# Opening by channel halves: the first adaLN modulation in two halves, and half of the SSM tiles' products ahead of the second half

## The chip, the core and the metric

One core of one Trainium2 chip runs the whole layer. The metric is the device time of one execution in microseconds (us), the median of the runs. Engines: TensorE (PE) multiplies and transposes, VectorE (DVE) and ScalarE (ACT) work element by element, GpSimd (POOL) splits weights, SyncE (SP) issues most DMAs; ACT issues DMAs too, in the order of its own instructions.

## What is computed

One decoder block on x (2048 rows of 1024 channels, float32), cut to what matters here:

```
c_act = silu(c)
sh1, sc1, g1, sh2, sc2, g2 = split(c_act @ w_ada + b_ada, 6)
h = rmsnorm(x, norm1_g) * (1.0 + sc1) + sh1
u_conv, u_ssm, gl_conv, gl_ssm = split(h @ w_in, ...)
y_conv = conformer_conv(u_conv, ...)
y_ssm = s5_mixer(u_ssm, a, b, c, d, log_dt, w_glu)
merged = sigmoid(gl_conv) * y_conv + sigmoid(gl_ssm) * y_ssm
x = x + g1 * (merged @ w_out)
h = rmsnorm(x, norm2_g) * (1.0 + sc2) + sh2
x = x + g2 * (swiglu(h @ w_ffn_in) @ w_ffn_out)
out = rmsnorm(x, final_g)
```

Nothing can be multiplied by `w_in` before `sh1` and `sc1` are known, and those need 8 MB of `w_ada`. This wait at the very beginning is the opening.

## The kernel before

The sequence is worked through in four blocks of 512 rows (mixers), then the feed-forward network in a second part that the change doesn't touch. Every float32 product is made of three: operand and weight are each split into a high part (fp32r) and the rest, and `three` (L1925) issues high x high, high x low, low x high. POOL makes the two parts of each 512 KB weight chunk (`w_hi`, L2255; `w_lo`, L2259) out of three raw buffers into two split slots. Each engine's order is written out by hand, and named steps on semaphores (`pe_pro`, L365; `act_pro`, L385) tie them.

The opening before, in the program's names:

- SP (L2313) issues eight 1 MB slabs of `w_ada` (`ada`, L2317), each one of two kinds (shift or scale), a half of the 1024 channels, and a half of the 1024 rows of the product. Then come three weight chunks (`raw`, L2367), small parameters (`load_small`), then further chunks.
- ACT issues the vectors (c, biases, gains; `nat_v`, L1263), x (`xs`, L1257), the SSM poles, `log_dt` and the B parameters (L1298 to L1302).
- `c` is turned by PE, copied to `vt` by DVE, and put through Silu by ACT (step `cs`). DVE puts it into `zc` (L658).
- Slabs 0, 2 and 4 are weighted and summed by DVE (`slab_sum`, L667 and L669); slabs 1, 3, 5, 6 and 7 go through PE (`modulation_rows`, L1852: four matmuls a slab, each recorded as two passes). PE adds DVE's sums (L1864), DVE copies the four rows of the result (`modrow`, L690), PE turns them (step `mt`, L1869), and DVE adds the bias and makes `scale0` (L693, L650, L652).
- PE turns x into eight channel tiles (`transposes`, L1882), with 32 small transposes of the B parameters between tile 3 and tile 4 (step `bx`, L1892). For each tile ACT makes the modulated high part and the full value (`h_tile`, L1292), and DVE the rest (`h_split`, L620).
- Then PE makes the four SSM input tiles `us0` to `us3`, each over all eight channel tiles (24 products), in order. ACT copies each one out (`uz`, L1391), stores it (L1395) and issues the loads that bring it back turned (`ssm_turn`: eight DMA issues a tile, L1400). In its program these stand as us0, us1, turn 0, us2, turn 1, us3, turn 2, turn 3. Behind them stand the sigmoid of the first convolution gate (L1406) and eight copies of the state matrices (L1324).
- PE goes on with two convolution input tiles (`ua0`, `ug0`) and the state matrices (`state_matrix`: L1906, L1911). Their transposes go through three banks, so PE waits there for ACT's copies. They read `wm`, which DVE builds after its last `h_split`, up to the copy of `cwt` (L752).

Of the kernel before, what the change touches and what calls it, by code (L numbers as in the profile page):

```python
# [45 lines left out]
def build(nc, x, c, w_ada, b_ada, norm1_g, w_in, conv_w, conv_b, conv_ln_g, conv_ln_b, conv_proj,  # L46
# [38 lines left out]
    FIRST_CHUNKS = [ssm_chunks + sum(conv_chunks, [])]  # L85
# [76 lines left out]
    with ExitStack() as ctx:  # L162
# [125 lines left out]
        def early(at, end, *buffers):  # L288
# [6 lines left out]
        jarg, jtmp, nat_v, nat_a, nat_w, iota_i, iota_f, cx = early(  # L295
            ssm_at, yn_at, ("jarg", [P, 2, T + 1, G]), ("jtmp", [P, T + 1, G]), ("nat_v", [nv_rows, P]),
            ("nat_a", [2 * G, P]), ("nat_w", [KC * TAPS, P]), ("iota_i", [P, NC + 1], I32),
            ("iota_f", [P, NC + 1]), ("cx", [P, 2, 4, P]))
# [5 lines left out]
        sv, jexp, jer, jei, b1, ptmp, modrow, zc, dvec, ddiag, zt, one_row, turns = early(  # L304
            mc_at, ms_at, ("sv", [P, 12, G]), ("jexp", [P, T + 1, G]), ("jer", [P, T + 1, G]),
            ("jei", [P, T + 1, G]), ("b1", [P, G, HG]), ("ptmp", [P, G, HG]), ("modrow", [4, HALF]),
# [4 lines left out]
            (ync_at, ync_at + 8192, ync_at + 16384, ms_at, ms_at + 8192, turn_at, turn_at + 8192, h_at))]  # L311
# [53 lines left out]
        pe_pro = ["v1", "ada1", "v0", "ada3", "ada5", "ada6", "ada7", "sums", "mt"] + h_steps[0:4] + ["bx"] + h_steps[4:] + ["v2"]  # L365
# [19 lines left out]
        act_pro = ["cs", "dt"] + norm_act + [f"nx{i}" for i in R(TT)] + ["ej", "m8", "sj", "cj"] + h_act  # L385
# [49 lines left out]
        for st, names in [("pro", pe_pro)] + list(enumerate(pe_mix)):  # L435
            z = 0
            for n in names:
                if n[:2] == "oc" or n[0] == "v" or n in ("bx", "sums"):
                    continue
                if st != "pro" and n[0] == "h":  # L440
                    plan[st, n] = 4 + int(n[1]) % 4
                elif is_z(n) or n[:2] == "o0":
                    plan[st, n] = z % 4
                    z += 1
# [105 lines left out]
        vectors_in = sem("vectors_in")  # L550
# [18 lines left out]
        for b, names in enumerate(pe_mix):  # L569
            chunk_used.append([tensor.after(b, n) for n in names if n[:2] in ("us", "gl", "ua", "ug", "oc")  # L570
# [8 lines left out]
        def _(dve):  # L579
# [34 lines left out]

            def wait_self(stage, name):
                dve.wait_ge(*vec.after(stage, name))
# [38 lines left out]
            dve.wait_ge(*tensor.after("pro", "v1"))  # L655
            link(v.tensor_copy(vt[:], bank[1][:, 0:nv_rows]), "vt")
            dve.wait_ge(*scal.after("pro", "cs"))
            link(v.tensor_copy(zc[:, :, 3], cact), "zc")  # L658

            def slab_sum(n):  # L660
                _, half, rows = SLABS[n]
                sums = acc[:, half * HALF:(half + 1) * HALF]
                dve.wait_ge(ada_in[n % ADA], 16 * (n // ADA + 1))
                for j in R(KD // 2):
                    k = rows * KD // 2 + j
                    if k == 0:
                        link(v.tensor_scalar(sums, ada[n % ADA][:, j, :], cact[:, k:k + 1], None, ALU.mult))  # L667
                    else:
                        link(v.scalar_tensor_tensor(out=sums, in0=ada[n % ADA][:, j, :], scalar=cact[:, k:k + 1],  # L669
                                                    in1=sums, op0=ALU.mult, op1=ALU.add),  # L670
                             f"slab{n}" if j == 3 else None)

            slab_sum(0)
            slab_sum(2)
            norm_mean("pro")
            slab_sum(4)
            norm_root("pro")
            dve.wait_ge(*tensor.after("pro", "v0"))
            link(v.tensor_copy(sv[:, 0:2, :].rearrange("p a g -> p (a g)"), bank[0][:, 0:2 * G]))
# [3 lines left out]
            link(v.tensor_tensor(lg, dt, ar, ALU.mult))  # L683
            link(v.tensor_tensor(jexp[:], iota_f[:, 0:T + 1].unsqueeze(2).broadcast_to([P, T + 1, G]),
                                 lg.unsqueeze(1).broadcast_to([P, T + 1, G]), ALU.mult))
            link(v.tensor_tensor(th, dt, ai, ALU.mult))
            reduce_angle(th, th, t0)
            angles(jarg[:, 0, :, :], jarg[:, 1, :, :], jtmp[:], th, T + 1, "jargs")
            dve.wait_ge(*tensor.after("pro", "sums"))
            link(v.tensor_copy(modrow[:], bank[7][0:4, :]), "modrow")  # L690
            dve.wait_ge(*tensor.after("pro", "mt"))
# [560 lines left out]
        def _(act):  # L1252
# [65 lines left out]
            for k in R(KD):  # L1318
                h_tile("pro", k, 0)
# [1243 lines left out]
```

## Time and profile before

| | |
|---|---|
| median of 3 runs | 2531.41 us (2530.98 to 2531.72) |
| profiled execution | 2529.16 us |
| span of its trace | 2527.4 us |
| PE busy | 2485.8 us, 98% |
| POOL busy | 1722.3 us, 68% |
| DVE busy | 1649.6 us, 65% |
| ACT busy | 876.1 us, 35% |

The busy share is an average over the span; the opening is its first 90 us. The chain of waits follows the work that ended last back from the end: each piece released the next, or stood before it on its engine. The timeline lists instructions by start. In both, a row begins with the start in us and the length in us; ACTq and SPq are queues that issue DMAs.

### The profile page before, as it was taken

How to read it: one execution, taken by the hardware profiler on the slowest of the kernel's cores; microseconds unless marked ns; L12 is line 12 of the kernel's file. 1: busy time of each engine (PE TensorE's matmuls, PEld its weight loads, DVE VectorE, ACT ScalarE, POOL GpSimd, SP SyncE). 2: the span in 40 equal slices, each digit the busy share in tenths (PEclk: the TensorE clock that was granted, in tenths of full speed). 3: DMA queues.
4: the chain of work that ended last, by engine and by line, in shares of the span. 5: the costliest groups of instructions: out<-in, count | busy, mean ns of one | idle time of the engine just before them, and what ended most of it. 6: DMA issues, size and time to landing. Idle time of an engine off the chain costs nothing.

```text
span 2527.4 us, 31370 instructions
## 1 busy us (share of the span) xinstructions
PE 2485.8 (98%) x11419; PEld 2047.8 (81%) x11419; DVE 1649.6 (65%) x2038; ACT 876.1 (35%) x1379; POOL 1722.3 (68%) x1182
## 2 busy tenths in 40 slices
PE   7999999999999999999999999999999999999998
PEld 3888788888888888888788888878888888888886
DVE  5899639946596648946833334385554326799798
ACT  4322421153012421146533345443323334445444
POOL 2777777677866777675787767788778764445545
PEclk9999999999999999999999999999999999999999
DMA  8676357553666347462332232325566327465533
GB/s 281 203 196 217 117 166 219 153 168 120 214 170 192 126 158 225 137 223 92 122 96 76 79 115 90 109 76 158 175 188 196 100 83 253 148 221 189 198 96 121
DMA packets 426161, 395.66 MB, mean 157 GB/s; under 512 B 92232, under 2 KB 330520, under 8 KB 424472
## 3 DMA queue, kind: packets, MB, share of 16 engines
q1 hardware_dynamic: 324688, 319.93, 40.5%
q10 hardware_dynamic: 101320, 73.72, 9.5%
q8 instruction: 92, 1.51, 0.2%
q14 instruction: 61, 0.50, 0.1%
HBM read 317.88 MB, written 67.24 MB: 152 GB/s over the span
## 4 chain that ended last, share of the span: by engine, by line
PE 84%; DVE 7%; DMA 3%; issue 2%; ACT 2%; POOL 1%; ACTq 1%; SPq 1%; POOLq 0%; DVEq 0%
PE bank L1927 19%; PE bank L1929 19%; PE bank L1928 19%; PE bank L2172 5%; PE bank L2173 5%; PE bank L2174 5%; DMA row_pair<-in_w_ffn_out 2%; PE bank L2086 2%; PE bank L2088 2%; PE bank L2087 2%; DVE bank L1027 1%; PE bank L2007 1%; PE bank L2006 1%; PE bank L1992 1%; DMA ada<-in_w_ada 1%
## 5 line engine op out<-in xcount | busy, mean ns | idle before, releaser
L2259 POOL TENSOR_TENSOR w_lo<-raw,w_hi 128x1024 fp32r<-128x1024 f32 x192 | 479.8, 2499 | 36.6 <-ACT w_hi L1385 12.5
L2255 POOL CAST w_hi<-raw 128x1024 fp32r<-128x1024 f32 x186 | 199.6, 1073 | 345.0 <-PE bank L1929 271.3
L1927 PE MATMUL bank<-h_hi,w_hi 128*128 128x512 f32 x896 | 351.8, 393 | 0.9 <-ACT wm L1324 0.9
L1929 PE MATMUL bank<-h_hi,w_lo 128*128 128x512 f32 x896 | 349.4, 390 | 0.0
L1928 PE MATMUL bank<-h_lo,w_hi 128*128 128x512 f32 x896 | 349.1, 390 | 0.0
L839 DVE SCALAR_TENSOR_TENSOR bank<-uc,cwt,bank 128x512 f32<-128x512 f32 x464 | 323.1, 746 | 6.2
L2282 POOL TENSOR_TENSOR fw_lo<-fsum,fw_hi 128x512 fp32r<-128x512 f32 x176 | 237.8, 1354 | 75.8 <-ACT fw_hi L1617 75.8
L1927 PE MATMUL bank<-xc_hi_T,fw_hi 128*128 128x512 f32 x704 | 276.4, 393 | 8.0 <-DVE tr L1032 6.5
L1929 PE MATMUL bank<-xc_hi_T,fw_lo 128*128 128x512 f32 x704 | 274.8, 390 | 0.0
L1928 PE MATMUL bank<-xc_lo_T,fw_hi 128*128 128x512 f32 x704 | 274.7, 390 | 0.0
L2309 POOL TENSOR_TENSOR ow_lo<-raw,ow_hi 128x512 fp32r<-128x512 f32 x116 | 161.8, 1395 | 163.1 <-ACT ow_hi L1664 163.1
L2172 PE MATMUL bank<-ow_hi,hid_hi 128*128 128x512 f32 x616 | 240.1, 390 | 3.2 <-POOL ow_lo L2309 3.1
L2174 PE MATMUL bank<-ow_lo,hid_hi 128*128 128x512 f32 x616 | 239.7, 389 | 0.0
L2173 PE MATMUL bank<-ow_hi,hid_lo 128*128 128x512 f32 x616 | 239.6, 389 | 0.0
L2282 POOL TENSOR_TENSOR fw_lo<-raw,fw_hi 128x512 fp32r<-128x512 f32 x110 | 156.0, 1419 | 80.7 <-ACT fw_hi L1617 80.6
L1927 PE MATMUL bank<-xc_hi_B,fw_hi 128*128 128x512 f32 x528 | 206.3, 391 | 2.4 <-DVE xc_lo_B L823 2.4
L1929 PE MATMUL bank<-xc_hi_B,fw_lo 128*128 128x512 f32 x528 | 205.5, 389 | 0.0
L1928 PE MATMUL bank<-xc_lo_B,fw_hi 128*128 128x512 f32 x528 | 205.4, 389 | 0.0
L1927 PEld LDWEIGHTS bank<-h_hi,w_hi 128*128 128x128 f32 x896 | 168.7, 188 | 35.6 <-issue 1.3
L1929 PEld LDWEIGHTS bank<-h_hi,w_lo 128*128 128x128 f32 x896 | 168.6, 188 | 35.7
L1928 PEld LDWEIGHTS bank<-h_lo,w_hi 128*128 128x128 f32 x896 | 168.7, 188 | 34.4
L1617 ACT ACTIVATE fw_hi<-fsum 128x512 fp32r<-128x512 f32 x176 | 110.8, 629 | 222.7 <-PE bank L1929 121.0
(341 smaller groups left out, 5242.8 us busy)
## 6 DMA issues: line engine op xcount, KB each, us to landing
raw<-in_w_in SPq DMA_DIRECT2D x112, 512.0 KB, 3.9
raw<-in_w_ffn_in SPq DMA_DIRECT2D x66, 512.0 KB, 5.7
hid_scratch<-tr SPq DMA_DIRECT2D x88, 256.0 KB, 3.2
raw<-tsum_scratch SPq DMA_DIRECT2D x66, 256.0 KB, 3.2
g2b<-in_w_ada SPq DMA_DIRECT2D x64, 256.0 KB, 3.7
ssm_m<-vk_scratch SPq DMA_DIRECT2D x32, 512.0 KB, 5.1
raw<-in_ssm_glu SPq DMA_DIRECT2D x32, 512.0 KB, 3.9
raw<-in_w_out SPq DMA_DIRECT2D x32, 512.0 KB, 3.6
```

What stands on the lines that cost most here:

```text
L839: ins = v.scalar_tensor_tensor(out=dst, in0=src, scalar=w, in1=conv_bank(m)[:], op0=ALU.mult, op1=ALU.add)
L1617: s.activation(fw_hi[i][:], src, ACT.Copy).then_inc(whi_done, 1)
L1927: t.matmul(dst, wh, xh, start=first, stop=False)
L1928: t.matmul(dst, wh, xl, start=False, stop=False)
L1929: return t.matmul(dst, wl, xh, start=False, stop=last)
L2172: t.matmul(dst, hid_hi[h][:, cols], ow_hi[w][:], start=(k == 0), stop=False)
L2173: t.matmul(dst, hid_lo[h][:, cols], ow_hi[w][:], start=False, stop=False)
L2174: return t.matmul(dst, hid_hi[h][:, cols], ow_lo[w][:], start=False, stop=(k == KH2 - 1))
L2255: g.tensor_copy(hi[:], src[:]).then_inc(hi_done, 1)
L2259: g.tensor_tensor(lo[:], src[:], hi[:].bitcast(F32), ALU.subtract).then_inc(split_done, 1)
L2282: g.tensor_tensor(fw_lo[i][:], part[WEIGHTS[i]], fw_hi[i][:].bitcast(F32), ALU.subtract)\
L2309: g.tensor_tensor(ow_lo[n % OW][:], fraw[n % 4][:, 0:HALF], ow_hi[n % OW][:].bitcast(F32), ALU.subtract)\
```

## The change

The slabs of the first channel half (0 to 3) are loaded and reduced first, giving shift and scale of channel tiles 0 to 3 (`scale00`); the second half (slabs 4 to 7, `scale01`) follows. The weights of the SSM tiles are cut anew: a chunk holds two SSM tiles (256 columns) over one half of the channel tiles. PE makes the products of us0 and us1 over channel tiles 0 to 3 (step `A0`), then slab 5 and the B transposes, then us2 and us3 over tiles 0 to 3 (`A1`), with the sums of the second half inside. After the second half's modulation `ssm_rest` makes us0 and us1 over tiles 4 to 7, then us2 and us3. Slabs 6 and 7 go from PE to DVE. ACT loads c alone and `log_dt` first, then x, then the vectors. A Silu on a constant stands ahead of the one on c.

```
-    FIRST_CHUNKS = [ssm_chunks + sum(conv_chunks, [])]
+    FIRST_CHUNKS = [[("us", pair_, half) for half in range(2) for pair_ in range(KS // 2)] + sum(conv_chunks, [])]
...
-        pe_pro = ["v1", "ada1", "v0", "ada3", "ada5", "ada6", "ada7", "sums", "mt"] + h_steps[0:4] + ["bx"] + h_steps[4:] + ["v2"]
+        pe_pro = ["vc", "ada1", "v1", "v0", "ada3", "sums0", "h0", "h1", "mt0", "h2", "h3", "A0", "ada5", "bx", "sums1", "A1",
+                  "mt1", "h4", "h5", "h6", "h7", "v2"]
...
-        act_pro = ["cs", "dt"] + norm_act + [f"nx{i}" for i in R(TT)] + ["ej", "m8", "sj", "cj"] + h_act
+        act_pro = ["pre", "cs", "dt"] + norm_act + [f"nx{i}" for i in R(TT)] + h_act[:2 * KH] + ["ej", "m8", "sj", "cj"]
+        act_pro += h_act[2 * KH:]
...
             slab_sum(0)
...
+            dve.wait_ge(*tensor.after("pro", "v1"))
+            for cols in (slice(0, 6 * KD), slice(7 * KD, nv_rows)):
+                link(v.tensor_copy(vt[:, cols], bank[7][:, cols]), "vt")
             dve.wait_ge(*tensor.after("pro", "v0"))
...
+            slab_sum(2)
+            norm_mean("pro")
...
+            modulation_half(0)
+            for k in R(KH):
+                h_split("pro", k)
+                slab_step(4, k)
+            slab_sum(6)
+            slab_sum(7)
...
+            modulation_half(1)
...
+            def ssm_products(pair_, k):
+                pe.wait_ge(*vec.after("pro", f"hl{k}"))
+                hi, lo = (w[pair_][:].rearrange("p (k n) -> p k n", n=2 * P) for w in (w_hi, w_lo))
+                for j in R(2):
+                    m, cols = 2 * pair_ + j, slice(j * P, (j + 1) * P)
+                    ins = three(bank[plan[0, f"us{m}"]][:], hi[:, k % KH, cols], lo[:, k % KH, cols],
+                                h_hi[:, k, :], h_lo[:, k, :], k == 0, k == KD - 1)
+                    if k == KD - 1:
+                        ins.then_inc(*tensor.step(0, f"us{m}"))
+                return ins
...
+            ssm_products(1, 0)
+            ssm_products(1, 1)
+            modulation_sums(1, [(0, "slab6", 1), (1, "slab7", 0)])
+            ssm_products(1, 2)
+            ssm_products(1, 3).then_inc(*tensor.step("pro", "A1"))
+            modulation_turn(1)
+            transposes("pro", 4)
+            pe.wait_ge(pro_v, mark["scale01"])
+            transposes("pro", 5)
+
+            def ssm_rest():
+                pe.wait_ge(split_done, RAW + 3)
+                for k in R(KH, KD):
+                    if k == KD - 1:
+                        pe.wait_ge(taps_in, 16 * KC)
+                        pe.wait_ge(*vec.after("pro", "hl7"))
+                        turn_rows_in(2, nat_w, bank[7])
+                    ssm_products(0, k)
+                    if k < KH + 2:
+                        transposes("pro", k + 2)
+                pe.wait_ge(split_done, RAW + 4)
+                for k in R(KH, KD):
+                    ssm_products(1, k)
...
-                    ssm_input(*R(KS))
+                    ssm_rest()
                     conv_input(0)
```

**PE, from the start to the first SSM product, before** (`nat_v` vectors, `ada` slabs, `nat_a` poles, `one_row` DVE's sums, `modrow` the modulation's rows, `xs` the transposes of x, `nat_b` the B parameters):

```order
L1841 MATMUL bank<-ident,nat_v 128x84
L1852 MATMUL bank<-ada_225,zc 4x512 x4
L1841 MATMUL bank<-ident,nat_a 128x64
L1852 MATMUL bank<-ada_227,zc 4x512 x4
L1852 MATMUL bank<-ada_229,zc 4x512 x4
L1852 MATMUL bank<-ada_230,zc 4x512 x4
L1852 MATMUL bank<-ada_231,zc 4x512 x4
L1864 MATMUL bank<-acc,one_row 4x512 x2
L1869 MATMUL bank<-ident,modrow 128x4 x4
L1882 MATMUL bank<-ident,xs 128x128 x16
L1892 MATMUL bank<-ident,nat_b_205 128x32 x16
...
L1927 MATMUL bank<-h_hi,w_hi_52 128x512
```

and in the change (a buffer's number may differ by one between the two; `ada_226` is slab 1):

```order
L1898 MATMUL bank<-ident,nat_c 128x8
L1879 MATMUL bank<-ada_226,zc 2x512 x4
L1870 MATMUL bank<-ident,nat_v 128x84
L1870 MATMUL bank<-ident,nat_a 128x64
L1879 MATMUL bank<-ada_228,zc 2x512 x4
L1886 MATMUL bank<-acc,one_row 2x512
L1918 MATMUL bank<-ident,xs 128x128 x8
L1893 MATMUL bank<-ident,modrow_217 128x2 x4
L1918 MATMUL bank<-ident,xs 128x128 x4
L1924 MATMUL bank<-h_hi,w_hi_52 128x512
```

Two slabs and one sum stand ahead of the first modulation in place of five and two, and products stand right behind three tiles' transposes.

**PE, between `A0` and the second half, in the change** (`w_hi_53` is the second split slot, with us2 and us3; the runs of 12 products each are shown by their first rows):

```order
L1879 MATMUL bank<-ada_230,zc 2x512 x4
L1945 MATMUL bank<-ident,nat_b_206 128x32 x16
L1945 MATMUL bank<-ident,nat_b_207 128x32 x16
L1924 MATMUL bank<-h_hi,w_hi_53 128x512
...
L1886 MATMUL bank<-acc,one_row 2x512 x2
...
L1893 MATMUL bank<-ident,modrow_233 128x2 x4
L1918 MATMUL bank<-ident,xs 128x128 x8
```

All of it now stands ahead of the transposes of channel tiles 4 to 7, which before followed the B transposes directly.

**SP, from the start, in the change** (before, the eight slabs stood ahead of `raw_49`, `raw_50` and `raw_51`):

```order
L2399 DMA ada_225<-in_w_ada 128x4x512
L2399 DMA ada_226<-in_w_ada 128x4x512
L2399 DMA ada_227<-in_w_ada 128x4x512
L2399 DMA ada_228<-in_w_ada 128x4x512
L2456 DMA raw_49<-in_w_in 128x4x256
L2456 DMA raw_50<-in_w_in 128x4x256
L2399 DMA ada_229<-in_w_ada 128x4x512
```

Two weight chunks moved ahead of four slabs.

## Rows read from the trace of the kernel before

**Rows 1.** The page, busy time of TensorE: busy us, share of the span, instructions.
```profile
PE 2485.8 (98%) x11419; PEld 2047.8 (81%) x11419; DVE 1649.6 (65%) x2038; ACT 876.1 (35%) x1379; POOL 1722.3 (68%) x1182
```
**Rows 2.** Chain of waits, 0 to 150 us: start us, us, what.
```profile
6.32 21.90 DMA ada<-in_w_ada
28.26 10.46 PE bank L1852 x24
...
43.58 3.64 PE bank L1892 x32
...
67.31 1.14 ACT uz L1391
...
72.28 1.67 ACTq L1400
...
83.26 1.28 ACT L1406
...
85.15 3.93 ACT wm L1324 x8
89.21 0.47 PE bank L1927
...
140.23 0.43 PE bank L1928
```
**Rows 3.** Timeline of ACT and its queue in the opening.
```profile
28.63 4.27 ACT L1311 ACTIVATE xs<-xs,rs 128x1024 f32<-128x1024 f32 x4 [2.55 <-DVE rs L630]
...
42.41 0.78 ACT L1292 ACTIVATE h_hi<-bank,mod,scale 128x512 fp32r<-128x512 f32 x1 [5.46 <-DVE scale L652]
...
56.42 1.14 ACT L1391 ACTIVATE uz<-bank 128x512 f32<-128x512 f32 x1 [2.70 <-PE bank L1929]
...
63.41 3.85 ACTq L1400 DMA_DIRECT2D u<-us_scratch  x8
...
75.53 7.70 ACTq L1400 DMA_DIRECT2D u<-us_scratch  x16
```
**Rows 4.** Timeline of DVE in the opening.
```profile
11.51 0.17 DVE L658 COPY zc<-vt 128x8 f32<-128x8 f32 x1 [2.28 <-ACT vt L1305]
...
16.32 3.11 DVE L669 SCALAR_TENSOR_TENSOR acc<-ada,vt,acc 128x512 f32<-128x512 f32 x4 [1.75 <-DMA ada<-in_w_ada]
...
40.55 0.68 DVE L690 COPY modrow<-bank 4x512 f32<-4x512 f32 x1 [6.79 <-PE bank L1864]
...
43.93 0.69 DVE L620 TENSOR_TENSOR h_lo<-bank,h_hi 128x512 fp32r<-128x512 f32 x1 [0.35 <-ACT bank L1292]
...
53.76 0.69 DVE L620 TENSOR_TENSOR h_lo<-bank,h_hi 128x512 fp32r<-128x512 f32 x1 [0.58 <-ACT bank L1292]
...
75.57 0.29 DVE L752 COPY cwt<-bank 128x124 f32<-128x124 f32 x1
```
**Rows 5.** Timeline of TensorE (PEld: its weight loads) in the opening.
```profile
11.74 5.94 PE L1852 MATMUL bank<-ada,zc 128*4 128x512 f32 x8 [2.87 <-DVE zc L658]
...
22.50 0.09 PEld L1852 LDWEIGHTS bank<-ada,zc 128*4 128x4 f32 x2 [4.74 <-DMA ada<-in_w_ada]
...
41.28 0.41 PE L1869 MATMUL bank<-ident,modrow 4*128 4x4 f32 x4 [0.84 <-DVE modrow L690]
41.62 1.97 PE L1882 MATMUL bank<-ident,xs 128*128 128x128 f32 x16
...
50.65 0.48 PE L1927 MATMUL bank<-h_hi,w_hi 128*128 128x512 f32 x1
...
83.43 1.03 PE L1906 MATMUL bank<-ident,cx 128*128 128x128 f32 x8
```
**Rows 6.** Timeline of POOL: the first weight chunk's cast.
```profile
34.94 1.04 POOL L2255 CAST w_hi<-raw 128x1024 fp32r<-128x1024 f32 x1 [32.09 <-DMA raw<-in_w_in]
```
**Rows 7.** Busy us (x) of PE, PEld, DVE, ACT, POOL; granted clock; DMA share, GB/s.
```profile
48.00:49.00 1.00, 1.00 (x7) 1.00 (x6) 0.93 (x3) 0.71 (x2) 0.00 (x0) 0.50 1.06 309
...
140.00:141.00 1.00, 1.00 (x4) 0.77 (x3) 0.97 (x2) 0.33 (x1) 1.00 (x2) 0.50 1.28 287
```

More of the change, by code:

```diff
@@ L653, in scale_of, with slab_step @@
                                      ALU.mult), f"scale{which}")
-            dve.wait_ge(*tensor.after("pro", "v1"))
-            link(v.tensor_copy(vt[:], bank[1][:, 0:nv_rows]), "vt")
             dve.wait_ge(*scal.after("pro", "cs"))
             link(v.tensor_copy(zc[:, :, 3], cact), "zc")
+            def slab_step(n, j):
+                kind, half, rows = SLABS[n]
+                part = (half + kind) % 2
+                sums = acc[:, part * HALF:(part + 1) * HALF]
+                k = rows * KD // 2 + j
+                if j == 0:
+                    dve.wait_ge(ada_in[n % ADA], 16 * (n // ADA + 1))
+                if k == 0 or n == 7 and j == 0:
+                    link(v.tensor_scalar(sums, ada[n % ADA][:, j, :], cact[:, k:k + 1], None, ALU.mult))
+                else:
+                    link(v.scalar_tensor_tensor(out=sums, in0=ada[n % ADA][:, j, :], scalar=cact[:, k:k + 1],
+                                                in1=sums, op0=ALU.mult, op1=ALU.add),
+                         f"slab{n}" if j == KD // 2 - 1 else None)
@@ L660, in slab_sum @@
             def slab_sum(n):
-                _, half, rows = SLABS[n]
-                sums = acc[:, half * HALF:(half + 1) * HALF]
-                dve.wait_ge(ada_in[n % ADA], 16 * (n // ADA + 1))
                 for j in R(KD // 2):
[L665 to L671, printed above, removed]
+                    slab_step(n, j)
@@ new lines, in _ @@
+            transposes("pro", 0)
+            transposes("pro", 1)
+            modulation_turn(0)
+            pe.wait_ge(*scal.after("pro", "cs"))
+            transposes("pro", 2)
+            pe.wait_ge(split_done, RAW + 1)
+            for k in R(KH):
+                if k == 1:
+                    transposes("pro", 3)
+                ins = ssm_products(0, k)
+            ins.then_inc(*tensor.step("pro", "A0"))
+            pe.wait_ge(pro_v, mark["vt"])
+            modulation_rows(5)
+            parameter_rows()
@@ L1923, in kernel_tiles @@
                     ins.then_inc(*tensor.step(0, f"kk{n}"))
-            def three(dst, wh, wl, xh, xl, first, last):
-                t.matmul(dst, wh, xh, start=first, stop=False)
-                t.matmul(dst, wh, xl, start=False, stop=False)
-                return t.matmul(dst, wl, xh, start=False, stop=last)
             def mixers(b, last=False):
-                chunk = [0]
+                chunk = [0 if b else KS]
                 def next_chunk():
@@ L2314, in _, with load_slab @@
         def _(sp):
-            for n, (kind, half, rows) in enumerate(SLABS):
+            def load_slab(n):
+                kind, half, rows = SLABS[n]
                 col = kind * D + half * HALF
@@ L2318, in _ @@
                     .then_inc(ada_in[n % ADA], 16)
+            for n in R(4):
+                load_slab(n)
             def load_small():
```

176 lines of the change are left out of this document (99 added, 77 removed).

## The prediction

> **What bounds the kernel now.** The page's busy shares come first: TensorE is busy 98% of the span [rows 1], so the change can only move idle or slow time of TensorE, and it touches nothing but the opening. The second view is the chain of waits over the first 150 us [rows 2]; the reader should watch who holds it. Up to 28.3 us it is the landing of the adaLN slabs, then 24 passes of slabs on PE (10.46 us, 0.436 each), then transposes, among them the 32 small ones of the B parameters (3.64 us). PE multiplies without a gap from 50.65 to 83.43 us [rows 5], but the chain leaves it at 67.31 for ACT: the copy of us2, its turning loads, us3, 16 more load issues up to 83.26, a sigmoid, eight state-matrix copies [rows 2, 3]. Only at 89.21 does PE go on. So two runners arrive at the state matrices almost together: PE at 83.43, ACT at 83.26 and with 6 us of work to do there. The prediction is about which of them the change helps.
>
> An opening that is x us shorter or longer shifts all that follows by x, since from 89.21 the chain is PE again and every later load, copy and split is timed by PE's steps.
>
> **The front: modulation of half the channels.** ACT issues one more DMA ahead (0.48, an eighth of a turn's 3.85) and a second Silu; c no longer waits for the other vectors. DVE's `zc`, 11.51 before, comes at about 12.4 [rows 3, 4]. x now comes in beside slabs 0 and 1, so I take 12.7 for slab 1 on PE (between 12.4, nothing lost, and 13.4). Slab 1 takes 5.94 [rows 5], to 18.6; the vectors and the poles are turned and copied behind it, 1.3, to 19.9. Seven small DVE operations at about 0.22 (a copy of 8 columns is 0.17 [rows 4], the rest handover), which stood later before, end at 21.4. Slab 2 on DVE is 3.11 [rows 4], to 24.5; mean, root, four small operations and the reciprocal take 1.4 at the same price, to 25.9. The scaling of x, 4.27 [rows 3], ends at 30.2; it began at 28.63 before, so this part gains 2.7. Slab 3 lands as before (22.5; the same bytes stand ahead of it [rows 5]) and was through at the latest when slab 5 began at 28.26 [rows 2]; with the sum that is 29.1, so x decides. Eight transposes are 1.0 (16 in 1.97), the turn 0.41 [rows 5], the copy of the rows lies beside the scaling (0.68 [rows 4]), bias and scale 0.6: ACT's first modulated tile starts at 32.4 against 42.41 [rows 3]. **Ten microseconds are won here**, and it is the last place where something is won. Slabs 4 to 7 are hidden now, and so are slabs 6 and 7, which leave PE (16 passes, 7.0 us) for DVE: eight operations at 0.78 behind the fourth rest end near 47, when PE is not yet at the sum.
>
> **First products (A0).** From ACT's first instruction on a tile to the end of DVE's rest is 2.2 us (42.41 to 43.93 + 0.69 [rows 3, 4]): 34.6. A product takes 0.228 on average (144 between 50.65 and 83.43 [rows 5]), six a channel tile 1.37. The transposes of tile 3 stand behind the first six, end at 36.5, and its rest is ready at 38.8; A0 would end at 40.2. But TensorE has stood nearly idle from 29 to 34.6, and the rows show what that does: behind the small transposes the granted clock is 0.50 [rows 7], 1.2 in place of 2.4 GHz, and there a product takes 0.43 [rows 2, 7]. I count one such spell, about nine products at 0.2 more: +1.8, A0 ends at 42.0. Bounds: none, 0; all 24 products, +4.9. The chunk for A0 is no wait: before it landed behind eight slabs at 34.94 [rows 6]; with half of the 8 MB behind it, it is some 10 us earlier, and POOL has nothing else to do.
>
> **What now stands between the two halves.** PE's order is fixed: slab 5, 8 x 0.436 = 3.5, to 45.5; B transposes 3.64, to 49.1 [rows 2]; 12 products 2.7, to 51.9; the sums, four passes, 1.7, to 53.6; 12 products 2.7, which cover the copy of the rows, to 56.3; turn 0.41, bias and scale 0.7, to 57.4. Then 2.2 for tile 4: 59.6. Before, the last tile, tile 7, was ready at 54.45 [rows 4].
>
> **The end of the SSM tiles.** Six products of tile 4 (1.37) and four transposes (0.5) stand ahead of ACT's tile 6, and the same again ahead of tile 7: 59.6 + 3.7 = 63.4, + 2.2 = 65.6 for the last rest. With the taps' transpose (0.3) and three products us0 is complete at **66.4; before, ACT took it at 56.42** [rows 3]. PE has 27 products left, 6.2, to 72.6, and 48 of the convolution tiles, 10.9: 83.5, what it was (83.43). PE neither gains nor loses.
>
> **ACT's queue decides.** Before, us0, us1, us2 and us3 came 5.5 us apart and ACT worked in between. Now us0 and us1 come together at 66.4 to 67.1 and all of its work stands behind: four copies and stores at 1.55 (1.14 for the copy [rows 3], and one issue, somewhat under a turn's 0.48), 6.2, and 32 issues, 3.85 + 3.85 + 7.70 = 15.4 [rows 3]: 66.5 + 21.6 = 88.1. Once in four turns one issue stood 1.67 in place of 0.45 [rows 2]; with that, 89.3. Before it was 83.26: **+4.8 or +6.1**. I take the latter, as the issues now stand closer together. The 6 us of sigmoid and state-matrix copies follow unchanged, so PE goes on at 95.3 in place of 89.21. DVE is late too, but less: from the last rest to `cwt` 21.4 (54.45 to 75.86 [rows 4]), so 87.0.
>
> The Trainium skill has a rule against such an order: "TensorE: Matmul & The Clock Gate", section "HAM oscillation — how this bites in real kernels", says that matmuls in short bursts between waits run at the low clock burst after burst. The trace agrees for one spell [rows 7]; that it recurs in every burst no row shows.
>
> **Sum.** The profiled execution took 2529.16, 2.3 below the median of 2531.41; +6.1 gives 2535.3 for such an execution and **2537.5** for the median. Changes below 0.2% (5.1 us) can't be told from none here.
>
> **The rivals.**
> - The same mechanism, but PE stays at the high clock or ACT's loads are issued without a stall: +3.1 to +4.9, about 2535.5. For it: the level stays up through shorter idle stretches. Against: 6 us with hardly a matmul. Chance 0.26.
> - **Not slower: a quick front.** If slab 1 runs at the high clock (3.5 in place of 5.94), all that hangs on the scaling of x comes 2.4 earlier; with no low spell (1.8) and no stall (1.2) us0 is complete at 62.2 and ACT free at 83.9: +0.7, 2532.1. It decides where us0 comes before 61.7; beyond that the gain is real. For it: slab 1's eight passes took 0.74 each, slab 5's 0.436 [rows 5, 2], so there is that much to win. Against: all three must hold. Chance 0.12, and 0.04 for more than 5 us faster, for which us0 would have to stand at 56.
> - Two low spells (A0 and behind the B transposes, where the trace has one [rows 7]), or the chunk for A0 late by 4, as if it didn't get ahead of the slabs: +8.5 to +10.5, about 2541. Chance 0.07.
> - Low clock in every burst: all 48 early products at 0.43 cost 9.7, 1.8 of them counted: +14, 2545.5. It is what the page's rule would make of it. Chance 0.03.
>
> The forecast itself, +5.1 to +8.5, has 0.48. Slower by over 0.2%: 0.48 + 0.07 + 0.03 = 0.58. Within: 0.26 + 0.12 = 0.38. Faster: 0.04. The range, 2531 to 2542, holds the first three cases and nearly all of the fourth; what it leaves out is about 0.12.
>
> **What would show it.** Right: first modulated tile near 32.4, A0 ending at 40 to 42, last rest at 64 to 67, us0's copy near 66.5, the turn issues without a wait between them up to 88 or 89, PE waiting some 5 to 6 us for ACT's state-matrix copies, and the trace from there the old one, shifted. Wrong: us0's copy before 62, PE at the state matrices later than ACT, or a chain of waits that doesn't pass through the turn issues. If the shift at the state matrices isn't the shift at the end, something later has slack that I didn't see.

## The result, and the profile after

The changed kernel takes **2552.88 us** (2550.18 to 2553.61) against 2531.29 (2530.98 to 2531.72) before: 1.0083 times, interval 1.0071 to 1.0096, 21.6 us slower. Slower was forecast, but by 6.1, and the time lies beyond the range. The profiled execution, the fastest of the four, has a span of 2548.3 us, 20.9 more than before. The page still has TensorE busy nearly all the time; the place to look is the opening.

The page's first row of the changed kernel:

```profile
PE 2489.6 (98%) x11410; PEld 2053.2 (81%) x11410; DVE 1674.1 (66%) x2051; ACT 876.7 (34%) x1380; POOL 1720.0 (67%) x1182
```

PE's timeline shows where the shift arises (start, duration, work, and in brackets the idle time before it and what ended it; L1918 transposes x, L1879 multiplies slabs, L1945 turns the B parameters, L1886 sums, L1924 multiplies):

```profile
35.08 1.97 PE L1918 MATMUL bank<-ident,xs 128*128 128x128 f32 x8 [4.98 <-ACT xs L1337]
...
40.63 0.77 PE L1924 MATMUL bank<-h_hi,w_hi 128*128 128x512 f32 x1 [2.02 <-DVE h_lo L629]
...
48.46 3.60 PE L1879 MATMUL bank<-ada,zc 128*2 128x512 f32 x8
51.99 3.73 PE L1945 MATMUL bank<-ident,nat_b 32*128 32x32 f32 x32
55.65 0.80 PE L1924 MATMUL bank<-h_hi,w_hi 128*128 128x512 f32 x1
...
61.07 2.06 PE L1886 MATMUL bank<-acc,one_row 128*2 128x512 f32 x4
...
72.02 0.77 PE L1924 MATMUL bank<-h_hi,w_hi 128*128 128x512 f32 x1 [3.87 <-DVE h_lo L629]
...
108.71 0.47 PE L1924 MATMUL bank<-h_hi,w_hi 128*128 128x512 f32 x1 [0.91 <-ACT wm L1353]
```

The first product stands at 40.63 where 50.65 was before [rows 5]: ten microseconds earlier, but six later than forecast. From there the lead is lost piece by piece, and PE's first product behind the state matrices comes at 108.71 in place of 89.21 [rows 2], **+19.5**. Another 1.5 is added where the state matrices are first used, around 153 to 163; from 298.88 (before 277.86) to the end the shift stays at 21. So 19.5 of the 21 are lost in the first 108 us.

What stands between the last rest and PE's next product is short to read. From DVE's timeline:

```profile
78.90 0.69 DVE L629 TENSOR_TENSOR h_lo<-bank,h_hi 128x512 fp32r<-128x512 f32 x1 [1.03 <-ACT bank L1316]
79.63 0.69 DVE L755 TENSOR_TENSOR b<-bank,sv 128x512 f32<-128x512 f32 x1
...
100.84 0.29 DVE L774 COPY cwt<-bank 128x124 f32<-128x124 f32 x1
```

and from ACT's:

```profile
94.68 7.72 ACTq L1429 DMA_DIRECT2D u<-us_scratch  x16
102.43 1.28 ACT L1435 ACT_TABLE_LOAD   x1 [8.17 <-issue]
```

The last rest ends at 79.59, 14.0 later than forecast. DVE needs 21.9 from its start to `cwt`, ACT has its four turns until 102.4; they end 1.3 apart, ACT last, and ACT's sigmoid and state-matrix copies follow. PE waits 3.42 for `cwt` up to 101.18, and then only 0.29 and 0.91 for ACT's copies. The tail behind the last rest was predicted: from its end to PE's next product 95.3 - 65.6 = 29.7 forecast, 108.71 - 79.59 = 29.1 measured. What stands ahead of it was not.

### What holds DVE

DVE's timeline of the changed kernel, where the first modulation is prepared:

```profile
25.81 0.88 DVE L634 TENSOR_SCALAR ss<-ss 128x4 f32<-128x4 f32 x1
26.61 0.18 DVE L710 TENSOR_TENSOR sv<-sv 128x32 f32<-128x32 f32 x1
26.82 2.32 DVE L711 TENSOR_TENSOR sv<-sv 128x32 f32<-128x32 f32 x1
29.18 0.94 DVE L712 TENSOR_TENSOR sv<-sv 128x32 f32<-128x32 f32 x1
30.16 0.35 DVE L713 RECIPROCAL sv<-sv 128x32 f32<-128x32 f32 x1
30.55 0.18 DVE L639 RECIPROCAL rs<-sd 128x4 f32<-128x4 f32 x1
30.64 2.18 DVE L715 TENSOR_TENSOR jexp<-iota_f,sv 128x288 f32<-128x288 f32 x1
```

and POOL's at the same time, casting and subtracting the first weight chunks:

```profile
25.41 1.26 POOL L2336 CAST w_hi<-raw 128x1024 fp32r<-128x1024 f32 x1 [22.56 <-DMA raw<-in_w_in]
26.76 2.34 POOL L2340 TENSOR_TENSOR w_lo<-raw,w_hi 128x1024 fp32r<-128x1024 f32 x1
29.04 1.04 POOL L2336 CAST w_hi<-raw 128x1024 fp32r<-128x1024 f32 x1
30.16 2.34 POOL L2340 TENSOR_TENSOR w_lo<-raw,w_hi 128x1024 fp32r<-128x1024 f32 x1
```

Three operations of equal size, L710 to L712, take 0.18, 2.32 and 0.94. The long ones end with POOL's operation: 26.82 + 2.32 = 29.14 against 26.76 + 2.34 = 29.10, and 29.18 + 0.94 = 30.12 against 30.08. They don't run slowly beside POOL; they wait for it. The two reciprocals, with one tensor to read, run beside POOL's second subtraction at the length that they have alone (0.35 and 0.18; in the run with the splits held, 0.35 and 0.18). Before, POOL's first cast came at 34.94 [rows 6], when DVE stood idle up to 40.55 [rows 4], so none of the rows read from before shows the clash. The change brings the chunk ten microseconds forward, into DVE's busiest stretch.

The Trainium skill, "SBUF — State Buffer", section "Who interferes with whom", states this as an exclusive lock on ports that the two engines share: a DVE instruction with two SBUF inputs contends with a GpSimd instruction that reads SBUF, and a DVE instruction with at most one SBUF input does not, unless it runs in a mode that uses both ports; of such a mode it says that the one that issues first keeps the ports for its whole instruction while the other is blocked. The rows above agree: the two ends above lie within 0.05 us, the reciprocals are free, and the one-input TENSOR_SCALAR L634, a form that by the section can run in such a mode, waits for the cast (25.81 + 0.88 against 25.41 + 1.26). The prediction did not weigh this section.

The second clash stands at tile 4's rest:

```profile
67.48 2.22 DVE L732 TENSOR_SCALAR sv<-jer 128x32 f32<-128x32 f32 x1
69.73 0.97 DVE L733 TENSOR_TENSOR sv<-sv 128x32 f32<-128x32 f32 x1
...
71.19 0.69 DVE L629 TENSOR_TENSOR h_lo<-bank,h_hi 128x512 fp32r<-128x512 f32 x1
```

```profile
67.30 2.35 POOL L2340 TENSOR_TENSOR w_lo<-raw,w_hi 128x1024 fp32r<-128x1024 f32 x1
69.62 1.03 POOL L2317 TENSOR_TENSOR acc<-g2b,vt 128x512 f32<-128x512 f32 x1
```

Four small operations, 0.2 each elsewhere, stand ahead of the rest on DVE. Two of them take 3.2, one up to the end of the subtraction of POOL's fourth split (69.65), the other up to the end of POOL's next operation (70.65); PE waits 3.87 for the rest.

### What the clock does

Windows of the changed kernel (busy us and counts of PE, PEld, DVE, ACT, POOL; granted clock; DMA share; GB/s):

```profile
34.00:44.00 10.00, 6.90 (x26) 5.50 (x27) 6.65 (x14) 5.12 (x7) 0.00 (x0) 0.51 0.84 262
44.00:54.00 10.00, 10.00 (x47) 6.10 (x45) 7.84 (x8) 5.42 (x8) 3.77 (x2) 0.98 1.00 309
54.00:62.00 8.00, 8.00 (x30) 5.56 (x30) 2.80 (x5) 0.00 (x0) 0.00 (x0) 0.57 0.20 59
...
71.00:76.00 5.00, 3.98 (x13) 3.24 (x14) 2.12 (x7) 0.44 (x1) 0.00 (x0) 0.66 0.49 154
...
100.00:106.00 6.00, 4.52 (x26) 4.12 (x27) 5.69 (x10) 3.35 (x5) 4.80 (x4) 0.72 0.64 175
...
153.00:163.00 10.00, 9.42 (x38) 8.94 (x39) 9.90 (x13) 2.23 (x4) 8.40 (x6) 0.53 0.90 238
```

The prediction counted one spell at 1.2 GHz, at the first products. There are three in the products (34 to 44, 55 to 61, 72 to 75) and one more at the state matrices' transposes (100 to 106). The price of the three by rows: transposes 1.97 in place of 1.0 and about seven products at 0.43 (the rest of A0 at 0.228); the first twelve products of A1 5.42 in place of 2.7; some six of tile 4.

### The profile page after: what moved, and what is told of

It reads as the page before. It is cut to its first block, busy times and chain, and to the rows that moved or that the text cites. A ratio compares the mean times of both kernels' runs of the same rounds, so it can differ in the third digit from the quotient of the medians.

```text
span 2548.3 us, 31381 instructions
## 1 busy us (share of the span) xinstructions
PE 2489.6 (98%) x11410; PEld 2053.2 (81%) x11410; DVE 1674.1 (66%) x2051; ACT 876.7 (34%) x1380; POOL 1720.0 (67%) x1182
## 4 chain that ended last, share of the span: by engine, by line
PE 83%; DVE 9%; DMA 3%; issue 2%; ACT 2%; POOL 0%; ACTq 0%; SPq 0%; POOLq 0%; DVEq 0%
PE bank L1924 19%; PE bank L1926 19%; PE bank L1925 19%; PE bank L2254 5%; PE bank L2253 5%; PE bank L2255 5%; DMA row_pair<-in_w_ffn_out 2%; PE bank L2167 2%; PE bank L2169 2%; PE bank L2168 2%; PE bank L2088 1%; PE bank L2073 1%; PE bank L2087 1%; DVE bank L1049 1%; DVE stage L841 1%
## 5 line engine op out<-in xcount | busy, mean ns | idle before, releaser
L1924 PE MATMUL bank<-h_hi,w_hi 128*128 128x512 f32 x896 | 354.7, 396 | 7.3 <-DVE h_lo L629 6.4
L1924 PE MATMUL bank<-xc_hi_T,fw_hi 128*128 128x512 f32 x704 | 276.1, 392 | 8.5 <-DVE tr L1054 7.1
L1924 PE MATMUL bank<-xc_hi_B,fw_hi 128*128 128x512 f32 x528 | 206.3, 391 | 2.5 <-DVE xc_lo_B L845 2.5
L1924 PEld LDWEIGHTS bank<-h_hi,w_hi 128*128 128x128 f32 x896 | 169.9, 190 | 43.8 <-issue 8.7
```

What stands on the lines that cost most here:

```text
L1924: t.matmul(dst, wh, xh, start=first, stop=False)
```

## The experiments

Each run was timed beside the kernel before on the same chip. The kernel before had a median of 2531.29 beside the change; 2529.42 beside the next four runs of the table; 2531.40 beside "no early products", "splits held, turns late" and the two "slab 6" runs without a held split; and 2530.09 beside the other four. So ratios compare better than times. "Last rest" is the start of tile 7's rest on DVE, "PE goes on" PE's first product behind the state matrices; both from each run's profile, while the time is the median of several executions, so small differences between neighbours mean little; that of "B transposes between products" took 2557.28, 6 above its median.

| kernel | time, us | ratio to before (interval) | last rest | PE goes on |
|---|---|---|---|---|
| before | 2531.29 | | 53.76 | 89.21 |
| changed | 2552.88 | 1.0083 (1.0071 to 1.0096) | 78.90 | 108.71 |
| POOL's splits held back | 2545.77 | 1.0064 (1.0049 to 1.0079) | 71.27 | 103.61 |
| DVE's order | 2549.44 | 1.0079 (1.0064 to 1.0094) | 73.58 | 105.71 |
| B transposes between products | 2551.19 | 1.0082 (1.0066 to 1.0099) | 81.56 | 112.36 |
| filler matmuls | 2551.46 | 1.0087 (1.0072 to 1.0102) | 76.95 | 109.68 |
| no early products | 2547.77 | 1.0064 (1.0050 to 1.0078) | 58.49 | 100.48 |
| splits held, turns late | 2542.10 | 1.0042 (1.0026 to 1.0057) | 71.50 | 101.95 |
| halves only, mended | 2542.70 | 1.0048 (1.0035 to 1.0062) | 61.57 | 98.78 |
| the same, splits held, turns late | 2540.50 | 1.0038 (1.0024 to 1.0052) | 60.24 | 97.77 |
| early products, all aids | 2547.54 | 1.0073 (1.0057 to 1.0088) | 72.15 | 100.17 |
| before, slab 6 on DVE | 2533.13 | 1.0006 (0.9998 to 1.0015) | 54.90 | 90.77 |
| the same, turns late | 2533.91 | 1.0016 (1.0007 to 1.0025) | 53.48 | 89.72 |
| slab 6 on DVE, split held | 2533.56 | 1.0008 (1.0000 to 1.0017) | 51.92 | 90.45 |

**POOL's splits held back.** Of the changed kernel, on POOL:

```diff
                     pool.wait_ge(raw_in[w % RAW], 16 * (b * (NW // RAW) + w // RAW + 1))
+                    if b == 0 and w == 0:
+                        pool.wait_ge(pro_v, mark["jargs"])
+                    if b == 0 and w == 3:
+                        pool.wait_ge(*vec.after("pro", "hl5"))
```

> POOL holds its first split back until DVE has the angles (step jargs), and the fourth until the rest of channel tile 5; nothing else is changed. Theory that DVE's small SBUF operations wait while POOL splits weights: the 2.34, 0.95 and 2.18 us of operations that elsewhere take 0.2 to 0.5 shrink to that, the scaling of x starts about 3.5 earlier (27.2 in place of 30.76), the rest of channel tile 4 follows its ACT output at once instead of 2 us later; together 4.5 to 6 us less than the change (2552.9), about 2547.5. Theory that those operations are long for a reason of their own (a handover, a DMA): no gain, or a loss of up to 3 us, because the weights of the first early products come later.

DVE's and POOL's timelines of this run:

```profile
25.90 0.19 DVE L711 TENSOR_TENSOR sv<-sv 128x32 f32<-128x32 f32 x1
26.13 0.19 DVE L712 TENSOR_TENSOR sv<-sv 128x32 f32<-128x32 f32 x1
...
26.84 0.43 DVE L715 TENSOR_TENSOR jexp<-iota_f,sv 128x288 f32<-128x288 f32 x1
```

```profile
30.43 1.04 POOL L2340 CAST w_hi<-raw 128x1024 fp32r<-128x1024 f32 x1 [27.58 <-DVE jarg L619]
```

The same operations take 0.19, 0.19 and 0.43 in place of 2.32, 0.94 and 2.18, and the last rest comes 7.6 earlier. It is the clash that cost this, and the time, 16.4 over its own runs of before in place of 21.6, fell by the 4.5 to 6 expected. Part of the clash only moved: POOL's splits, now behind the angles, hold the two operations that make the scale, which took 0.17 and 0.16 in the change.

```profile
33.01 0.92 DVE L693 TENSOR_SCALAR scale<-mod 128x4 f32<-128x4 f32 x1
33.96 0.94 DVE L694 TENSOR_TENSOR scale<-scale,vt 128x4 f32<-128x4 f32 x1
```

PE goes on only 5.1 earlier, because here ACT ends last: its turns run to 96.4 with `cwt` ready at 93.49.

**DVE's order.** POOL as in the change; DVE's pole operations go behind slab 7, and tile 4's and 5's rests ahead of the small operations:

```diff
-            link(v.tensor_tensor(den, t0, t1, ALU.add))
-            link(v.reciprocal(den, den))
...
             slab_sum(7)
+            link(v.tensor_tensor(den, t0, t1, ALU.add))
+            link(v.reciprocal(den, den))
...
+            h_split("pro", 4)
+            h_split("pro", 5)
             link(v.tensor_scalar(nr, e_r, -1.0, None, ALU.add))
```

> Only DVE's order: the four operations on the poles go from ahead of the root's reciprocal to behind slab 7, and the rests of channel tiles 4 and 5 go ahead of the six small operations; POOL is as in the change. Theory that operations on DVE are held up while POOL splits: the reciprocal of the root (four columns) comes behind the mean directly, near 27 in place of 30.55, unless it is held up itself, and tile 4's rest ends 2 us sooner: 4 to 6 us less than the change, about 2548. The held-up time then turns up in the next operations, the angles, where it costs nothing up to 35. If only the order counts and not POOL, the gain is the plain length of the moved operations, 1.0 + 0.9 us.

Scaling of x starts at 26.96 in place of 30.76, but the angles are now what waits (jexp, with two SBUF inputs, 2.36; L606, a TENSOR_SCALAR, 2.35), and `modrow` comes at 34.99 (35.86 in the change). PE goes on 3.0 earlier than in the change; the intervals of the two ratios overlap, so the expected 4 to 6 are not shown. A new order among DVE's operations moves the wait to the next one.

**B transposes between products.** They are issued eight at a time, ahead of each of A1's first four triples of products, so that no stretch holds small transposes alone:

```diff
-            parameter_rows()
+            eight = parameter_rows()
...
-            ssm_products(1, 0)
-            ssm_products(1, 1)
+            ssm_products(1, 0, eight)
+            ssm_products(1, 1, eight)
```

> The 32 small B transposes go in groups of eight between the first four groups of three products of us2 and us3, in place of one run of 32 ahead of them. Theory that the run lets the granted clock fall: it stays at 1.00 from 45 on, the twelve products take 0.228 in place of 0.43 and the four passes of the sums 0.436 in place of up to 0.85; PE is at the turn of the second half 3.0 us earlier; 3 to 4 us less than the change, about 2549.5. Theory that the clock falls there for what went before: no gain within 1 us.

Windows of this run:

```profile
45.00:55.00 10.00, 10.00 (x44) 5.64 (x42) 9.68 (x11) 3.55 (x6) 3.73 (x2) 1.00 0.96 295
55.00:65.00 10.00, 10.00 (x30) 4.70 (x29) 1.27 (x3) 0.00 (x0) 0.00 (x0) 0.50 0.01 3
```

The low clock came all the same, at 55, and stayed through the sums. Mixing did not keep it away, and the time stayed that of the change; the idea fell.

**Filler matmuls.** Seven slab matmuls whose result nobody reads, ahead of A0:

```diff
+            filler(5)
             transposes("pro", 0)
...
             transposes("pro", 2)
+            filler(2)
```

> Seven matmuls of 512 columns into a bank that is not yet in use are added: five ahead of the transposes of channel tile 0, two behind those of tile 2, where PE waits for ACT and DVE. Theory that idling lets the clock fall ahead of the early products: granted clock 1.00 up to 52, eight transposes 1.0 in place of 1.97, the first nine products 0.228 in place of 0.43, A0 ends 2.5 to 3.5 us earlier, and the total falls by as much, about 2550. If the first early products are paced by ACT and DVE anyway, A0 ends at most 1 us earlier. If the fillers themselves delay, up to 1 us slower.

The granted clock stays at 1.00 from 27 to 53, A0 ends 2.05 earlier (slab 5 at 46.41 against 48.46), and the last rest 1.95 earlier. So about 2 is what the first spell costs. At the state matrices it is spent again: 0.52 from 98 to 108, where the change had 0.83; PE goes on 1.0 later, and the time did not fall.

**No early products.** The halves stay; the us tiles stand whole behind the second, as before:

```diff
-            pe.wait_ge(split_done, RAW + 1)
-            for k in R(KH):
-                ins = ssm_products(0, k)
...
-            ssm_products(1, 0)
-            ssm_products(1, 1)
...
-                    ssm_rest()
+                    ssm_input(*R(KS))
```

> The modulation stays in two halves, but no product is multiplied ahead of the second half: the us tiles stand whole behind it, in the order of the kernel before. If the early products are what is lost (they run at the low clock in short bursts, and the four us tiles come together, so that DVE and ACT have everything still to do behind the last rest): slab 5 follows the transposes of tile 3 on PE at about 38 to 39, sums near 48, tile 4's rest near 56, the last rest near 61 in place of 78.90, products without a gap from 56 on, first tile past the state matrices near 95 (before 89.21, after 108.71), time 5 to 8 over the kernel before, about 2537. If the split of the modulation itself costs the time (DVE held beside POOL's splits at the front, sums over half the channels twice), the last rest comes no earlier than 70 and the time stays over 2545.

The last rest comes 20 earlier than in the change and PE goes on 8.2 earlier, though this edit had a fault of its own: the taps' transpose waited for the last rest ahead of all products and held them to 59.46. The time, 16.4 over the kernel before, is far from the 5 to 8 expected.

**Splits held, turns late.** The run with POOL's splits held, and on ACT:

```diff
-                    ssm_turn(2)
-                    ssm_turn(3)
                     sigmoid_u(0)
                     state_matrix()
+                    ssm_turn(2)
                     angle_turns()
                     sigmoid_u(1)
+                    ssm_turn(3)
```

> The run with POOL's first splits held back, with one thing more: ACT's third and fourth turn (two copies and 24 load issues) stand behind the state-matrix copies. Queue theory: in the run with the splits held back, cwt was ready at 93.20 but ACT issued turning loads up to 96.42 and copied from 97.7; now ACT is free near 84, the copies start near 95.5 and PE's next products come 2 to 4 earlier than at 103.61: time about 2543. If DVE's state matrices alone decide, or the loads are needed sooner than they now come, no gain: 2545 to 2547, with a new wait for u in the stage at 150 us.

PE goes on 1.7 earlier than with the splits alone, a little under the 2 to 4 expected, and the time, 2542.10, is close to the 2543 of the queue theory: ACT's turns are part of the tail as soon as DVE is early enough. PE now waits for `cwt` again, 3.42 up to 93.78, and the state matrices' transposes behind it take 1.97 and 5.50 where the kernel before had 1.03 and 4.00: the granted clock is 0.50 from 93 to 98. From PE's start on them to its next product it is 8.2 here and was 5.8 before, so 2.4 of the gain went there.

**Halves only, mended.**

```diff
-            turn_rows_in(2, nat_w, bank[7])
...
                             pe.wait_ge(*vec.after("pro", f"hl{k}"))
+                            if k == KD - 1:
+                                turn_rows_in(2, nat_w, bank[7])
```

> The run without early products once more, with one fault of its own mended: there the turning of the taps waited for the last rest ahead of all products, and held the first from about 55 to 59.46; now it stands ahead of the eighth channel tile's products. If that wait was on the path: first product near 56, us0 3 earlier, PE's next products after the state matrices at 97 to 98 in place of 100.48, time about 2544. If DVE's front and the low clock are all that is left of the loss: no change at 2547.

PE's timeline of this run:

```profile
59.66 0.78 PE L1923 MATMUL bank<-h_hi,w_hi 128*128 128x512 f32 x1
...
93.11 1.03 PE L1973 MATMUL bank<-ident,cx 128*128 128x128 f32 x8
93.98 3.90 PE L1978 MATMUL bank<-ident,wm 128*128 128x128 f32 x32
98.78 0.47 PE L1923 MATMUL bank<-h_hi,w_hi 128*128 128x512 f32 x1 [0.91 <-ACT wm L1352]
```

The first product is no earlier than with the fault (expected near 56): in this execution POOL's first split again held the pole operations (2.32 and 0.94), the scaling of x began at 30.83, and the last rest came 3.1 later than in the run before. From 59.66 to 93.11 PE doesn't wait once; `cwt` (83.51) and ACT's turns (to 91.9) are hidden behind it. This is the comparison that decides: **the change without its early products costs 9.6, the early products another 9.9** (98.78 - 89.21, 108.71 - 98.78; by the medians, each against its own runs of before, 12.6 and 9.0). The first part is not the halves alone: the new order of loads and slabs 6 and 7 on DVE belong to it, and the clash at the front. The second holds the weight chunks' new cut as well.

**The same, splits held, turns late.** Both edits from above on this one.

> The run before this one with POOL's first split held until the angles are done and ACT's third and fourth turn behind the state-matrix copies. Port theory: the angles of 288 columns, which took 2.01, 1.17 and 2.35 beside POOL's splits, take 0.46 and 0.31 again, modrow stands 3 earlier than 34.60, the first modulated tile near 33.5, the last rest near 56; with the queue out of the way PE's next products after the state matrices come at 92 to 94, time 2535 to 2537: the split of the modulation alone, at its best, 4 to 6 over the kernel before. If halving the modulation were worth its name, it would come under 2531.

The scaling of x starts 3.9 earlier (26.97 against 30.83), the last rest only 1.3. Windows of this run and, for the same stretch, of the run with halves only:

```profile
46.00:60.00 14.00, 11.42 (x45) 6.94 (x45) 7.50 (x21) 5.38 (x8) 0.00 (x0) 0.52 0.53 166
```

```profile
46.00:60.00 14.00, 11.19 (x58) 7.53 (x58) 9.40 (x23) 5.31 (x9) 0.00 (x0) 0.67 0.62 190
```

Most of the gain at the front was given back, in two parts. The splits, now behind the angles, hold DVE's two scale operations here too (0.93 and 0.94 in place of 0.17 and 0.16), 1.5. And PE's slab 5 (5.95 in place of 4.92) and sums (3.57 in place of 2.9) run at the low clock for longer, about 1.5 as well. The expected 2535 to 2537 was missed by 3.5.

**Early products, all aids.** Held splits, DVE's order, fillers and late turns in the changed kernel.

> The changed kernel, early products and all, with every aid that gained in its opening: POOL's splits 0 and 3 held back, DVE's pole operations behind slab 7 and tile 4's and 5's rests ahead of the small operations, seven filler matmuls ahead of the first products, ACT's third and fourth turn behind the state-matrix copies. If the losses add up as named (port 5, clock at the first products 2, queue 2 to 3): last rest near 68 in place of 78.90, PE's next products at 98 to 100 in place of 108.71, time 2539 to 2541, so still over the run without early products. If the low clock only moves to another place when it is driven out of one: no better than 2542.1, the run with splits and turns alone.

PE goes on at 100.17, close to the 98 to 100 expected, but the last rest, 72.15, missed the 68, because the aids get in each other's way. POOL's fourth split, released by tile 5's rest, now meets the small operations that DVE's new order puts right behind that rest, and tile 6's rest comes at 71.32, behind them:

```profile
67.35 2.44 POOL L2350 TENSOR_TENSOR w_lo<-raw,w_hi 128x1024 fp32r<-128x1024 f32 x1
```

```profile
67.58 2.26 DVE L738 TENSOR_TENSOR sv<-sv 128x32 f32<-128x32 f32 x1
69.87 0.97 DVE L739 TENSOR_TENSOR sv<-jei,sv 128x32 f32<-128x32 f32 x1
```

At the front x is scaled by 30.19, but PE works on the first five fillers from 30.26 to 34.65 and turns x only then. The time, 2547.54, is 6 or more above the 2539 to 2541 expected. The 11.0 by which PE goes on later than before have become 16.2 by 294; PE waits 2.03 at 256.85 and 1.54 at 269.57, where the change has no such wait. PE's timeline:

```profile
256.85 0.50 PE L1924 MATMUL bank<-ys_hi,w_hi 128*128 128x512 f32 x1 [2.03 <-DVE ys_lo L629]
```

So this run doesn't show that the named losses add up, and something more is lost later. The late turns alone are not it, since the run with splits and turns shows no such wait there; which of the edits makes these waits isn't settled.

**Three runs on the kernel before**, to measure the clash where nothing else of the change is present. Slab 6 goes from PE to DVE, behind the angles:

```diff
             angles(jarg[:, 0, :, :], jarg[:, 1, :, :], jtmp[:], th, T + 1, "jargs")
+            slab_sum(6)
...
-            for n in R(5, 8):
-                modulation_rows(n)
+            modulation_rows(5)
+            modulation_rows(7)
```

> The kernel before with one thing taken from the change: slab 6 of the adaLN weights goes from PE to DVE, eight operations of 0.78 behind the angles, where DVE stood idle up to 40.55. PE then has 24 passes in place of 32 behind 22.5 (8 x 0.436 = 3.5 less) and waits for the landing of slab 7. If PE's passes set the end of the modulation: mt and all behind it about 2 earlier, time about 2529 against 2531.3, 0.1% less. If the landing of the last slab or DVE decides: no change. If DVE's eight operations are held by POOL's splits as in the changed kernel: 1 to 3 slower.

With the turns late as well:

> The run before this one, and ACT's third and fourth turn behind the state-matrix copies. In the kernel before PE was through at 83.43 and ACT at 83.26 with the copies still to do, so PE waited until 89.21. Queue theory: ACT's copies now start as soon as cwt is there (75.86), and PE goes on without the gap of some 5: with slab 6 moved, 3 to 7 below the kernel before, 2524 to 2528. If the turned loads are then needed sooner than they come, or the copies wait for PE's transposes which stand behind the convolution tiles, no more than the run before.

Nothing of this came. ACT is free early and waits 7.39 for PE, PE is at the state matrices at 84.04 and goes on at 89.72, 5.7 later, as before (83.43 and 89.21, 5.8). So the 6 us there are not ACT's queue: PE's own transposes (1.04 and 3.90) and the last copy fill them, and they follow whichever of PE, `cwt` and ACT comes last.

With POOL's first split waiting for slab 6 instead:

```diff
+                    if b == 0 and w == 0:
+                        pool.wait_ge(pro_v, mark["slab6"])
```

> The kernel before with slab 6 on DVE, and POOL's first split held until slab 6 is added up. Without that wait DVE's four operations of slab 6 took 5.73 in place of 3.1, beside POOL's first split, and the kernel came out 1.7 over the one before. Port theory: slab 6 takes 3.1, modrow stands 1.5 to 2.5 earlier than there (41.65), time 2529 to 2531, some 2 to 3 below that run. If something else slowed DVE (the landing of the slab): 5.73 again and 2533.

DVE's timeline without and with that wait:

```profile
34.73 5.73 DVE L669 SCALAR_TENSOR_TENSOR acc<-ada,vt,acc 128x512 f32<-128x512 f32 x4
```

```profile
33.32 3.12 DVE L669 SCALAR_TENSOR_TENSOR acc<-ada,vt,acc 128x512 f32<-128x512 f32 x4
```

The clash is 2.6 on the same four operations. But the kernel without it there, with `modrow` 2.2 earlier than before (38.36 against 40.55), is no faster. POOL's second split now holds DVE's scale (0.94) and one of the operations behind it (2.51), so that the first rest comes at 44.35 where it was 43.93 [rows 4]. The last rest is still 1.8 earlier, but the products start at 49.51 in place of 50.65 and run at 0.43 up to 53.5, since the low stretch, which ended near 51 before, lasts to 53.5 here. Its us0 is copied at 57.20, before at 56.42 [rows 3]. Windows of this run:

```profile
44.00:47.00 3.00, 2.35 (x18) 1.77 (x17) 2.79 (x9) 3.00 (x5) 0.00 (x0) 0.97 1.15 348
47.00:53.00 6.00, 5.64 (x17) 4.44 (x18) 5.32 (x15) 4.88 (x8) 0.00 (x0) 0.50 0.91 279
```

None of the three, nor any other run, beats the kernel before.

## Why the prediction was wrong

- **Right:** that the time won at the front is lost again, that everything behind the last rest is passed on to the end (forecast tail 29.7, measured 29.1; 6.1 forecast, and a last rest 14.0 later than forecast, make the 19.5 at the state matrices but for 0.6), and that PE waits at the state matrices for what hangs on the last rest, not for its own products. Who holds PE was half right: the forecast has ACT's turns end 2.3 behind `cwt` (89.3 and 87.0), and they end 1.3 behind it (102.40 and 101.13); but PE's one long wait is for `cwt`, and the chain of waits passes through DVE's operations from 79.63 to 101.13 and not through the turn issues, which the prediction had named as a sign of being wrong. The 1.2 that it added for one slow issue did not come: the turns took 3.75, 3.89 and 7.72.
- **The front failed first.** "Ten microseconds are won here" was to hold at the first modulated tile; it starts at 38.27 where 42.41 was before [rows 3], 4.1 won. The step that failed reads: seven small DVE operations at about 0.22, slab 2, then "mean, root, four small operations and the reciprocal take 1.4 at the same price, to 25.9". The reciprocal ended at 30.73. Of these 4.8, 1.2 is the poles' landing (their copy ends at 21.08 in place of 19.9), and 3.6 is DVE waiting for POOL, shown by the run with the splits held (its reciprocal ends at 26.92, its poles' copy 0.2 earlier). Another 1.0 up to the first modulated tile, 38.27 in place of 32.4, is transposes and turn at the low clock; the forecast's own terms add up to 32.2. The prices were taken from rows where POOL was idle, and the prediction itself moved POOL's work: "with half of the 8 MB behind it, it is some 10 us earlier, and POOL has nothing else to do". POOL's earlier start was booked as a gain and never asked whom it meets.
- **The clock was counted once.** "I count one such spell, about nine products at 0.2 more: +1.8." The first spell alone measured 2.0 at A0's end (filler run); the twelve products behind the B transposes, at 2.7 in the sum, took 5.4, and tile 4's were low as well: 4 to 5 more than forecast on the way to the last rest. The rival with low clock in every burst, chance 0.03, comes nearest of all, at 2545.5, but by luck: twelve of A1's products and most of A0's ran at 0.228, and it knew nothing of POOL. The row that the prediction gave for its spell, 48 to 49 [rows 7], stands behind small transposes and not behind idle time; that idle time ahead of the first products brings the low clock there is shown by the filler run.
- **Tile 4's rest.** "Then 2.2 for tile 4: 59.6" left out that small DVE operations stand ahead of it; beside POOL's fourth split they, and the scale's L693 (0.56 in place of 0.17), cost 2.6. Without POOL they would have been hidden behind ACT's work on the tile, as in the run with halves alone (0.18 to 0.19 each, DVE idle 1.09 behind them). The program showed their place.
- The sum at the last rest's end, 79.59 in place of 65.6: first modulated tile 5.9, A0 0.6 (48.46 for 42.0), up to the second turn 3.2 (65.98 for 56.3), tile 4's rest 2.6 (71.88 for 59.6), the last rest 1.7; together 14.0. One part remains open: in the run with halves alone, how much of its 9.6 is low clock and how much the longer order of slab 5, B transposes, sums and turn between the halves. Nearly all of it, 9.0, stands ahead of the first product (59.66 for 50.65); slab 5 and the sums take 4.92 and 2.9 there, where eight and four passes at 0.436 would take 3.5 and 1.7. The fillers show the clock's price at one place only; no run kept it high throughout.

## What to carry to other kernels

When a change brings a load forward, follow the engine that consumes it: here POOL's splits landed on DVE's small operations, and an operation of 0.19 us took 2.32. Price small operations by who else runs then, not by the row where they stood alone. Holding the load's consumer back is no cure by itself: in three runs the held split met the next DVE operations instead. And a gain in front of short, broken work on TensorE is no gain yet: in three runs (fillers, halves with the splits held, slab 6 with the split held) a part of the 2 to 4 us won ahead came back as work at half the clock.

## What the runs showed of the hardware

- DVE operations with two inputs in SBUF, and TENSOR_SCALAR with one, wait for the end of POOL's cast or subtraction, whatever their own size: 32 columns 2.32 and 0.94, 288 columns 2.18, slab sums of 512 columns 5.73 for four in place of 3.12, a TENSOR_SCALAR of 4 columns 0.88 in place of 0.17. A reciprocal with one input (0.35, 0.18) did not.
- The granted clock fell although PE's row shows no idle time: in the changed kernel PE is busy 10.00 of 10.00 us from 44 to 54, with A0's last products, the slab matmuls with two columns of weights and the 32 small transposes, and the clock falls from 1.00 to 0.50 between 54.4 and 54.8; with the transposes mixed among products it falls at 55.
